# Local attention in two layers of a hybrid decoder: the value products and the normalisation rearranged

## The reference

```python
s = jnp.einsum('bnqkgd,bnskd->bnkgqs', qb, kk) * (hd ** -0.5)      # blocks of 128 queries, 256 keys
s = jnp.where(valid, s, NEG_INF)                                   # band of 128, causal
m = jnp.maximum(jnp.max(s, axis=-1, keepdims=True), sink)
p = jnp.exp(s - m)
p = p / (jnp.sum(p, axis=-1, keepdims=True) + jnp.exp(sink - m))
o = jnp.einsum('bnkgqs,bnskd->bnqkgd', p, vv)
```

## Time and profile before

| | us |
|---|---|
| median of 3 runs (lowest, highest) | 1453.86 (1453.58, 1456.06) |
| the profiled execution | 1452.88 |
| its span | 1451.1 |
| PE busy, matmuls | 1431.3 (99%) |
| VectorE busy | 1162.2 (80%) |
| ScalarE busy | 977.7 (67%) |

### The profile page before, as it was taken

One profiled execution on the slowest core, in us unless ns is written; L12 is line 12 of the kernel. 1 busy time (PEld: TensorE's weight loads), 2 busy tenths in 40 slices (PEclk: granted clock), 3 DMA queues, 4 the chain that ended last, 5 costly groups with the idle time before them and its releaser, 6 DMA issues.

```text
span 1451.1 us, 17969 instructions
## 1 busy us (share of the span) xinstructions
PE 1431.3 (99%) x6814; PEld 1186.6 (82%) x6814; DVE 1162.2 (80%) x1322; ACT 977.7 (67%) x1430; POOL 67.9 (5%) x93
## 2 busy tenths in 40 slices
PE   8999999999999999999999999999999999999997
PEld 6887888888888888888888778888888888888885
DVE  7999756798768768898798986468987778689985
ACT  6777666769756647676577775668696666576763
POOL 0000000000000000000000000000000000000000
PEclk9999999999999999999999999999999999999999
DMA  9998738775668777788849776467865787768871
GB/s 367 267 291 236 276 130 276 243 232 178 173 221 262 219 301 245 238 281 250 300 144 279 251 214 250 196 208 265 234 171 196 229 246 232 307 198 267 259 233 44
DMA packets 49397, 341.42 MB, mean 235 GB/s; under 512 B 5568, under 2 KB 6208, under 8 KB 8608
## 3 DMA queue, kind: packets, MB, share of 16 engines
q1 hardware_dynamic: 37392, 259.54, 47.5%
q0 software_dynamic: 8912, 63.84, 22.9%
q10 hardware_dynamic: 3008, 16.90, 2.9%
HBM read 332.91 MB, written 7.34 MB: 234 GB/s over the span
## 4 chain that ended last, share of the span: by engine, by line
PE 83%; DVE 10%; DMA 3%; issue 2%; ACT 1%; SPq 0%; POOLq 0%; POOL 0%; DVEq 0%; ACTq 0%
PE bank L763 25%; PE bank L765 24%; PE bank L764 24%; DVE w_lo L1566 5%; PE bank L820 3%; DMA raw_b<-in_stream 3%; DVE w_lo_more L1566 2%; PE bank L997 1%; PE bank L1098 1%; PE bank L1080 1%; PE bank L971 1%; PE bank L983 1%; DMA raw<-in_stream 1%; DVE raw L1563 1%; PE bank L995 0%
## 5 line engine op out<-in xcount | busy, mean ns | idle before, releaser
L1566 DVE TENSOR_TENSOR w_lo<-raw,w_hi 128x1024 fp32r<-128x1024 f32 x342 | 402.3, 1219 | 133.4 <-ACT w_hi L1171 133.2
L1171 ACT ACTIVATE w_hi<-raw 128x1024 fp32r<-128x1024 f32 x342 | 342.9, 1053 | 168.2 <-PE bank L765 136.1
L763 PE MATMUL bank<-w_hi,hT_lo 128*128 128x512 f32 (+1 forms) x696 | 274.3, 394 | 2.7 <-DVE half L1669 1.9
L765 PE MATMUL bank<-w_lo,hT_hi 128*128 128x512 f32 (+1 forms) x696 | 268.3, 386 | 0.0
L764 PE MATMUL bank<-w_hi,hT_hi 128*128 128x512 f32 (+1 forms) x696 | 267.9, 385 | 0.0
L763 PEld LDWEIGHTS bank<-w_hi,hT_lo 128*128 128x128 f32 x696 | 130.9, 188 | 32.1 <-DVE half L1669 2.8
L765 PEld LDWEIGHTS bank<-w_lo,hT_hi 128*128 128x128 f32 x696 | 130.8, 188 | 26.7
L764 PEld LDWEIGHTS bank<-w_hi,hT_hi 128*128 128x128 f32 x696 | 131.1, 188 | 24.4
L763 PE MATMUL bank<-w_hi,S_lo 128*128 128x512 f32 x364 | 144.9, 398 | 1.3 <-ACT snap L1252 0.9
L765 PE MATMUL bank<-w_lo,S_hi 128*128 128x512 f32 x364 | 142.1, 390 | 0.0
L764 PE MATMUL bank<-w_hi,S_hi 128*128 128x512 f32 x364 | 141.9, 390 | 0.0
(11 more groups left out here) (227 smaller groups left out, 2436.3 us busy)
## 6 DMA issues: line engine op xcount, KB each, us to landing
raw<-in_stream SPq DMA_DIRECT2D x150, 1024.0 KB, 6.1
raw_b<-in_stream SPq DMA_DIRECT2D x38, 1024.0 KB, 6.7
raw_q<-in_stream SPq DMA_DIRECT2D x38, 1024.0 KB, 6.9
raw<-in_stream POOLq DMA_DIRECT2D x34, 1024.0 KB, 9.0
raw_x<-in_stream SPq DMA_DIRECT2D x18, 1024.0 KB, 6.8
raw_b<-in_stream POOLq DMA_DIRECT2D x16, 1024.0 KB, 10.8
raw_q<-in_stream POOLq DMA_DIRECT2D x8, 1024.0 KB, 9.3
raw<-in_stream SPq DMA_DIRECT2D x8, 256.0 KB, 7.1
```

The lines of the kernel that those rows point to most:

```text
L763: nc.tensor.matmul(dst, xl, wh[:, a:b], start=first, stop=False, skip_group_check=more)
L765: return nc.tensor.matmul(dst, xh, wl[:, a:b], start=False, stop=last, skip_group_check=more)
L1171: nc.scalar.activation(slots(o)[0][:, part], raw_slot(s)[:, part], ACT.Copy).then_inc(hi_split, 1)
L1566: nc.vector.tensor_tensor(lo[:, part], raw_slot(s)[:, part], hi[:, part].bitcast(F32), ALU.subtract)\
```

## The change

- `grp_values`: the 64 columns of `sv` become the stationary operand, and `pT` moves. Even heads write PSUM partitions 0 to 63, odd heads 64 to 127 of the same bank: 2 products of 512 columns for the first value tile, 2 of 256 for the second. The result comes out transposed.
- So the probabilities are normalised ahead of it, in a new step `n` g: VectorE adds the sink and takes the reciprocal, ScalarE scales `prob` in place, 8 instructions, and `pt` g waits for these.
- `st` falls away. In `pv` g ScalarE writes `bT_hi` and VectorE `bT_lo` from the bank.
- `grp_transposes` takes the pieces head by head.
- `stA` is lent as a staging slot (`raw_a`) between the transposes of mk and the projection mq. The window of `raw_b` in the mixing part now ends with pv0.
- `SCHEDULE`, three of the `FFN_ORDER` lists in several places and the fourth in a few, `S_AFTER` and `ADDED` are other ones.

```diff
@@ SCHEDULE
-mk0.1+xt0 mk1.0+xt1 mk1.1 sq1.0 skv.0 mkt S_sum S_hi S_lo sq0.0 skt sq0.1 sq1.1 mv0.0 sqt mv0.1 s0 rk:5 mv1.0 e0 s1 rk:3 mv1.1 rk:1 e1 pt0 rv0.0 rk:6 pv0 pt1 rk:7 rk:2 s2 mv_out rk:4 rg:5 e2 pv1 rotq rv0.1 s3 rg:1 rv1.0 rg:3 rotk pt2 rg:6 rqt rv1.1 e3 rkt pv2 rg:2 rg:7 mq1.0 rg:4 gs:5 pt3 gs:1 gs:3 rs gs:6 pv3 gs:2 st mq1.1 gs:7 ro re gs:4 gr:1 us0.0 us0.1 mq0.0 mq0.1 us1.0 gr:5 mqt mkT_in gr:3 us1.1 rt gr:6 gr:2 gr:7 ur0.0 ur0.1 gr:4 gm:5 ms me mv_in gm:1 ur1.0 mn gm:3 ur1.1 mpt gm:6 mpv gm:2 gm:7 um0.0 gm:4 x_in um0.1 um1.0 mg0 um1.1 wo0.0 mg1 wo1.0 wo0.1 wo1.1+yt0
+mk0.1+xt0 mk1.0+xt1 skv.0 mk1.1 sq0.0 S_sum S_hi S_lo mkt sq0.1 sq1.0 skt sq1.1 mv0.0 sqt rk:5 s0 mv0.1 rk:3 e0 s1 mv1.0 mv1.1 e1 n0 n1 rk:1 rv0.0 pt0 rk:6 pv0 pt1 rk:7 mv_out rk:2 s2 rk:4 rg:5 pv1 e2 n2 rotq rv0.1 s3 rv1.0 rg:3 rqt rg:1 pt2 e3 rotk rg:6 rg:2 pv2 rv1.1 rg:7 n3 mq1.0 rkt rg:4 gs:5 pt3 gs:3 rs gs:1 gs:2 pv3 mq1.1 gs:6 ro gs:7 re us0.0 gs:4 us0.1 mq0.0 gr:1 gr:5 mq0.1 us1.0 mqt us1.1 rt mkT_in gr:3 gr:6 gr:2 ur0.0 gr:7 ur0.1 gr:4 ms gm:5 me mv_in ur1.0 mn gm:3 gm:1 ur1.1 mpt gm:6 mpv gm:7 gm:2 um0.0 gm:4 um0.1 um1.0 x_in mg0 um1.1 wo0.0 mg1 wo1.0 wo0.1 wo1.1+yt0
...
@@ FFN_ORDER: 4 orders, neighbours swapped; the first of them:
-u0.0 u0.1 u1.0 g0 u1.1 d0 p0:1 g1 p0:5 p0:3 p0:6 d1 p0:2 p0:7 p1:5 p0:4 g3 p1:3 g2 p1:1 d3 p1:6 p1:2 p1:7 p2:5 d2 p1:4 p2:3 g4 p2:1 g5 p2:6 p2:2 d4 p2:7 p3:5 p2:4 p3:3 g7 p3:1 d5 p3:6 d7 p3:7 g6 p3:2 p3:4 d6 u10.0 g9 u10.1 g8 d9 d8 g10 mix d10
+u0.0 u0.1 u1.0 g0 u1.1 d0 p0:1 g1 p0:5 p0:3 p0:6 d1 p0:2 p0:7 p1:5 p0:4 g3 p1:3 g2 p1:1 d3 p1:6 p1:2 p1:7 p2:5 d2 p1:4 p2:3 g5 p2:1 g4 p2:6 p2:2 d5 p2:7 p3:5 p2:4 p3:3 p3:1 d4 g7 p3:6 d7 g6 p3:7 p3:2 d6 g9 p3:4 u10.0 u10.1 g8 d9 d8 g10 mix d10
...
-S_AFTER = {(0, 1): (1, 2, 3), (0, 2): (0, 1, 2), (1, 1): (0, 1, 3), (1, 2): (0, 1, 2)}
+S_AFTER = {(0, 1): (0, 2, 3), (0, 2): (0, 1, 2), (1, 1): (0, 1, 4), (1, 2): (0, 1, 2)}
...
-ADDED = {(0, 'gm'): (6, 7, 4), (0, 'gr'): (7, 4), (0, 'gs'): (7, 4), (0, 'rg'): (6, 7, 4), (0, 'rk'): (6, 7), (1, 0): (7, 4), (1, 1): (6, 7, 4), (1, 2): (7,), (1, 3): (6, 7, 4), (2, 0): (6, 7), (2, 1): (6, 7, 4), (2, 2): (7, 4), (2, 3): (7, 4)}
+ADDED = {(0, 'gm'): (6, 7, 4), (0, 'gr'): (7, 4), (0, 'gs'): (6, 7), (0, 'rg'): (6, 7, 4), (0, 'rk'): (6, 7, 4), (1, 0): (7, 4), (1, 1): (6, 7, 4), (1, 2): (7,), (1, 3): (6, 7, 4), (2, 0): (7, 4), (2, 1): (6, 7, 4), (2, 2): (7, 4), (2, 3): (7,)}
...
-RAW_B, RAW_Q, RAW_X = (3, 4), (5, 6), 7
+RAW_B, RAW_Q, RAW_X, RAW_A = (3, 4), (5, 6), 7, 8
 X_ITEMS = AT[0]["mix", UNIT_AT["mk1", 0]] + 4, AT[0]["mix", UNIT_AT["wo0", 0]] - 6
-_st = STEPS.index(("step", "st"))
-_after_st = next(s for s in STEPS[_st:] if s[0] != "step")
-B_ITEMS = (max(AT[0]["mix", UNIT_AT[c, 1]] for c in ("mv0", "mv1")) + 5,
-           AT[0][_after_st if _after_st[0] == "prod" else ("mix", _after_st[1])] + 1)
+
+
+def item_after(name):
+
+    s = next(s for s in STEPS[STEPS.index(("step", name)):] if s[0] != "step")
+    return AT[0][s if s[0] == "prod" else ("mix", s[1])]
+
+
+B_ITEMS = max(AT[0]["mix", UNIT_AT[c, 1]] for c in ("mv0", "mv1")) + 5, item_after("pv0") + 1
+MQ_ITEM = AT[0]["prod", 0, "mq", 5] if "mq" in PAIRS[0] else min(AT[0]["mix", UNIT_AT[c, 1]] for c in ("mq0", "mq1"))
+A_ITEMS = item_after("mkt") + 4, MQ_ITEM + 1
...
+    if PAIRS[0] and A_ITEMS[0] < i < A_ITEMS[1]:
+        slots.append(RAW_A)
...
+        raw_a = new("raw_a", [P, UW], at=a_at)
...
-        SPLIT_TO = {"rt": (G_RET, bT_hi, bT_lo), "st": (None, bT_hi, bT_lo), "mpv": (None, bT_hi, bT_lo)}
+        SPLIT_TO = {"rt": (G_RET, bT_hi, bT_lo), "mpv": (None, bT_hi, bT_lo)}
...
+                if s == RAW_A and (owner is None or o // NI != owner // NI):
+                    sp.wait_ge(*full(o // NI, "mkt_3"))
...
                 def grp_transposes(g):
-                    pe.wait_ge(swa_exp, l * NGRP + (g + 1))
+                    pe.wait_ge(swa_probs, l * NGRP + (g + 1))
                     for j in range(3):
                         name = f"pt{g}_{j}"
                         pe.wait_ge(*room(l, name))
                         for i in range(4):
-                            head, col = (i, 0) if j == 0 else (2 * (j - 1) + i // 2, WIN * (1 + i % 2))
+                            head, part = divmod(4 * j + i, 3)
                             last = nc.tensor.transpose(bank(name)[:, i * P:(i + 1) * P],
-                                                       prob[:, g % 2, head, col:col + P], ident[:, :])
+                                                       prob[:, g % 2, head, part * P:(part + 1) * P], ident[:, :])
                         last.then_inc(fullsem(name), 1)
 
                 def grp_values(g):
@@ -989,13 +1003,16 @@
                     name = f"pv{g}_0"
                     wait_out(l, [f"pt{g}_{j}" for j in range(3)], [name])
                     pe.wait_ge(*room(l, name))
-                    for i in range(GRP):
-                        v = [sv[:, t, kv * HD:(kv + 1) * HD] for t in range(TT)]
-                        o = bank(name)[:, 2 * i * HD:2 * (i + 1) * HD]
-                        nc.tensor.matmul(o[:, 0:HD], pT[:, i, :], v[0], start=True, stop=True)
-                        for t in range(TT):
-                            last = nc.tensor.matmul(o[:, HD:2 * HD], pT[:, GRP + 2 * i + t, :], v[t],
-                                                    start=t == 0, stop=t == TT - 1)
+                    heads = pT[:, :, :].rearrange("p (j o c) q -> p j o c q", j=2, o=2)
+                    for t in range(TT):
+                        v = sv[:, t, kv * HD:(kv + 1) * HD]
+                        for odd in range(2):
+                            o = bank(name)[odd * HD:(odd + 1) * HD, :].rearrange("p (j b q) -> p j b q", j=2, b=TT)
+                            if t == 0:
+                                nc.tensor.matmul(o, v, heads[:, :, odd, 0:2, :], start=True, stop=False, skip_group_check=True)
+                            else:
+                                last = nc.tensor.matmul(o[:, :, 1, :], v, heads[:, :, odd, 2, :], start=False, stop=True,
+                                                        skip_group_check=True)
                     last.then_inc(fullsem(name), 1)
...
-                    elif s == "st":
-                        wait_out(l, [f"pv{g}_0" for g in range(NGRP)], ["st_0"])
-                        for j in range(4):
-                            transpose_to(l, f"st_{j}", token_major(stA), 2 * j)
...
-                    need = {"us": "st", "ur": "rt", "um": "mpv"}
+                    need = {"us": "pv{0}_0", "ur": "rt_{0}", "um": "mpv_{0}"}
...
-                            pe.wait_ge(*out_of(l, f"{need[chunk[:2]]}_{j}"))
+                            pe.wait_ge(*out_of(l, need[chunk[:2]].format(j)))
...
+                    if kind == "mq" and PAIRS[0]:
+                        act.wait_ge(weights_made, last_read(l, [RAW_A], *A_ITEMS))
...
-                        if s == "st" and PAIRS[0]:
-                            act.wait_ge(weights_made, last_read(l, RAW_B, *B_ITEMS))
...
+                    elif s in ("n0", "n1", "n2", "n3"):
+                        g = int(s[1])
+                        act.wait_ge(swa_sums, l * NGRP + (g + 1))
+                        for i in range(GRP):
+                            for b, (c0, c1) in enumerate(((0, WIN), (WIN, 3 * WIN))):
+                                p = prob[:, g % 2, i, c0:c1]
+                                last = nc.scalar.activation(p, p, ACT.Copy, scale=ssum[:, g % 2, i, b:b + 1])
+                        last.then_inc(swa_probs, 1)
+                    elif s in ("pv0", "pv1", "pv2", "pv3"):
+                        if s == "pv0" and PAIRS[0]:
+                            act.wait_ge(weights_made, last_read(l, RAW_B, *B_ITEMS))
+                        hi_parts(l, f"{s}_0", bT_hi, 2 * int(s[2]), None)
...
-                    elif s in ("pv0", "pv1", "pv2", "pv3"):
-                        g = int(s[2])
+                    elif s in ("n0", "n1", "n2", "n3"):
+                        g = int(s[1])
                         par = g % 2
                         dve.wait_ge(swa_exp, l * NGRP + (g + 1))
                         own(nc.vector.tensor_tensor(ssum[:, par], ssum[:, par], sexp[:, par], ALU.add))
                         settled()
-                        own(nc.vector.reciprocal(ssum[:, par], ssum[:, par]))
-                        settled()
-                        name = f"pv{g}_0"
-                        dve.wait_ge(*full(l, name))
-                        for t in range(TT):
-                            o = bank(name)[:, :].rearrange("p (h b d) -> p h b d", h=GRP, b=2)[:, :, t, :]
-                            dst = stA[:, t, GRP * HD * g:GRP * HD * (g + 1)].rearrange("p (h d) -> p h d", h=GRP)
-                            i = nc.vector.tensor_tensor(dst, o, ssum[:, par, :, t:t + 1].broadcast_to([P, GRP, HD]), ALU.mult)
-                        i.then_inc(free(name), 1)
```

(21 more changed lines are left out.)

6 lines of the change are left out of this document (3 added, 3 removed).

## The result

The changed kernel takes 1463.48 us in the median of its runs (1461.28 to 1466.44), the kernel before 1453.89 us in the same session; the ratio is 1.0064, with a 95% interval of 1.0044 to 1.0084. That is 9.6 us slower, above the 1455.1 us of the forecast and outside its range. The profiled execution took 1463.71 us, its span is 1461.6 us.

What follows compares the result with a forecast made beforehand. PE, busy 99% of the span, was taken to bound the kernel: -7.1 - 3.5 + 11.8 = +1.2 us on 1452.88 gives 1454.1, a median of 1455.1 us. Its own range was 1451 to 1458, the overall range 1443 to 1461.

Steps and rivals of the forecast that it cites:

- Values: Local attention's value products: a group falls from 2.62 to 1.73 us, column halves side by side; eight groups, -7.1 us.
- halves in a row: Rival on the value products: the column halves don't work side by side, 3.02 us a group, 1465.4 us; chance 8%.
- program order: Rival on the value products: four passes take the time of three, 2.37 us a group, 1460.2 us; chance 7%.
- Removed work: PE work gone from the value products (-7.1 us) and the `st` transposes back (-3.5 us), together -10.6 us.
- Price of n: ScalarE's eight new scaling instructions per attention group: 2.8 us a group, 22 us in all.
- The first group: First attention group: PE loses 1.1 us at pt0 and 4.8 at pv0, 5.9 us; 11.8 with layer 1.
- T: PE's end of mv1.1 in the first attention group, 276.65 us in the kernel before; ScalarE's queue is counted from it.
- Staging and other orders: Changed staging slots, FFN orders and `ADDED`: each taken as 0, with ends -1 and +4, and -2 and +2.
- it ends when it did: First FFN: PE's 3.5 us wait for `gT_lo` keeps the same instructions ahead of it, so its end doesn't move.
- the rest are swaps of neighbours: Order changes beyond the moved sums of `x` and the exchange in `ADDED` only swap neighbouring items; taken as 0.
- I carried the same count through the other groups ... Nothing there.: Later attention groups: n2 and n3 have 11 and 12 us of PE work before pt2 and pt3, so no wait.
- the clock: Rival: PE's clock falls in the 4.8 us wait at pv0, 1.5 us per wait, 1458 us; chance 10%.

Runs made afterwards that it cites:

- x7: The changed kernel with both heads of a pair written to the same 64 PSUM rows, half the attention output not computed: 1468.12 us, ratio 1.0095.
- x1: The changed kernel with each n step's eight scalings cut to one of one element, probabilities not normalised: 1441.37 us, ratio 0.991.
- x8: The kernel before with the changed `FFN_ORDER` and `S_AFTER`, its own `ADDED` kept: 1452.38 us, ratio 0.9988.
- x2: The kernel before with the changed `FFN_ORDER`, `S_AFTER` and `ADDED`, its own `SCHEDULE` and attention kept: 1474.56 us, ratio 1.0137.
- x13: The changed kernel with n's scaling kept for groups 2 and 3, one element for groups 0 and 1: 1453.79 us, ratio 0.9996.
- x4: The changed kernel with n0, n1, n2, pt1 and gs:1 at other places in `SCHEDULE`: 1458.69 us, ratio 1.0031.
- x5: The changed kernel with n0, n1, gs:1 moved, n2 ahead of s3, pv0 behind rk:7, pt1 behind rk:2: 1459.37 us, ratio 1.0034.
- x6: The changed kernel, same orders, with n's scaling done by VectorE as two products over four heads: 1440.78 us, ratio 0.9902 to the kernel before.

## Why the prediction was wrong

Right, step by step:

- *Values.* From the end of the matmul ahead to the start of the next one's regular pace, a later group is 0.09 + 1.44 + 0.11 = 1.64 us against 1.73 forecast and 2.62 before. The rivals "halves in a row" and "program order" (3.02 and 2.37 us) are out, by this row and by x7. The rule that matmuls start and end strictly in program order (the Trainium skill, "TensorE: Matmul & The Clock Gate", "Part 3: Packing small matmuls — row/col tiling") was read in the prediction so that only one pass of four lies beside another; eight passes in 1.44 us are all in pairs (1.30 us without ends), so that reading is wrong here. The rows don't tell which passes make a pair, so they don't decide whether the rule itself fails or the order of the passes is another than the prediction took.
- *Removed work.* 8 x 0.98 + 3.5 = 11.3 us of PE against 10.6 forecast. x1, in which n is almost free, gained 13.0 us over before, 11.2 of them in mixing, so the rest of the change costs nothing in the sum; a wait of 0.8 us at pv0 stays in each layer. VectorE is 5.1 us less busy against 6.
- *Price of n.* 5.62/2 = 2.8 us a group, as forecast.
- *The first group.* pt0 began 1.0 us late (1.1 forecast), and pv0 began 18.0 us after T (T = 276.75 here, 294.73) against 18.2. But PE's wait did not come as one of 4.8 us at pv0. It was split, in idle time: 0.9 at pt0, 1.8 at rk:6, then 1.15 at pv0 (2.4 in layer 1). That is 3.9 and 5.1 us against 5.9. The eviction of rk:1's bank is a term of the prediction's queue, but nobody was taken to wait for it.
- *Staging and other orders*, taken as 0: the stages outside mixing changed by -1.5 us together, in x1 as in the changed kernel. For the FFN orders x8 supports it. The first FFN's stall of 3.5 us came as 1.6 us for `act_g` and 1.0 for `gT_lo` and ended at 35.5 us instead of 36.0, so "it ends when it did" was nearly right. (The view of the earlier trace rows also has a wait of 2.0 us at the kernel's opening, above "1.9 us and less"; it is the same in both kernels.) `ADDED` is neutral only together with its schedule (x2), so "the rest are swaps of neighbours" was true of the whole and not of the part.

Wrong: **the sentence "I carried the same count through the other groups ... Nothing there."** The count was carried only to the `pT` copies. Behind each n in ScalarE's queue stand also the evictions that give PE its next bank, and those are due much sooner: n2 has 11 us until pt2, but PE asked for rv0's bank 1.5 us after n2 began (321.04 less 2.02, against 317.55). It cost 2.0 us at rv1.0 and 2.3 at gs:3 in each layer, 8.6 us of waits. x13 shows that these waits need nothing of the first groups: the two steps that I had taken as free cost 12.4 us by themselves, as much as the 12.0 us of the two that I had counted.

The second term too small is the clock, a rival with 10% and 3 us (1.5 per wait). It fell, but not in one long wait, and beside the other cause. The windows (PE, PEld, DVE, ACT and POOL busy, granted clock, DMA) of the changed kernel: behind the wait at rk:6 and around that at rv1.0 in layer 0, then over pt0, rk:6, pv0 and rv1.0 in layer 1:

```profile
291.00:293.00 2.00, 2.00 (x7) 1.48 (x5) 2.00 (x3) 2.00 (x4) 0.00 (x0) 0.50 0.00 0
...
315.00:330.00 15.00, 12.97 (x60) 10.13 (x59) 12.62 (x24) 9.54 (x24) 0.86 (x1) 0.89 0.85 227
...
1004.00:1060.00 56.00, 48.88 (x255) 37.81 (x253) 45.32 (x62) 46.04 (x94) 2.59 (x3) 1.00 0.77 207
```

And around the wait at rv1.0 in x13, layer 0 and layer 1:

```profile
315.00:330.00 15.00, 14.62 (x74) 12.33 (x75) 12.78 (x18) 10.85 (x14) 0.87 (x1) 1.00 0.62 147
...
1025.00:1040.00 15.00, 12.98 (x60) 10.17 (x59) 12.62 (x24) 9.52 (x22) 0.86 (x1) 0.89 0.83 216
```

So the same waits of one kernel brought the fall in one layer and not in the other: in the changed kernel it came behind rk:6 and rv1.0 in layer 0 and behind gs:3 in layer 1, in x13 behind rv1.0 in layer 1 alone. At 0.50, the 1.2 GHz level, a matmul of 512 columns takes 0.43 us instead of 0.23. Over the kernel that is about 4.3 of the 6.1 us by which PE is busier than in x1.

The sum corrected, in spans of the profiled executions: -11.2 for what x1 gained in mixing, nearly all PE's removed work, and -1.5 outside it; then +15.8 of waits behind n, +1.3 of other waits, and +6.1 by which PE is busier, clock and edges of waits together. That is +10.5, the difference of the spans (1461.6 and 1451.1). The medians say +9.6, which is within what single runs differ by. The mechanism, work saved on PE and given back through ScalarE's queue, was right. Its size was not, since only one kind of customer of that queue was counted.

What stays open: what let the clock fall behind a wait in one layer and not behind the same wait in the other, and whether any order makes n on ScalarE as cheap as on VectorE. x4 and x5 found none, and both moved the steps by hand.

## What to carry to other kernels

When work is put into an in-order queue, list everything that stands behind it and ask of each who waits for it and when, the release of a bank first: a consumer that is due in 1.5 us counts more than the one 11 us away that the new work is meant for. An engine that is 67% busy can be the wrong one and one that is 80% busy the right one: eight small instructions in front of evictions cost 22 us here, and two wide ones on the busier engine nothing that could be measured (1440.8 us in x6, 1441.4 in x1), though whether the engine or the two wide instructions did it was not separated. A table of what comes by which way (`ADDED`) and the schedule that it was made for are one edit; apart, they cost 22 us in x2.
